# A hybrid decoder step: four experts of 32 slots on four column groups in one phase, decode attention on two column groups

## What is computed

```
s = jnp.einsum('nthe,nshe->nhts', qn_b, kn) + jnp.einsum('nthe,nse->nhts', qr_b, kr)
p = jax.nn.softmax(s, axis=-1).astype(ckv.dtype)
return jnp.einsum('nhts,nsr->nthr', p, ckv)
```

```
pg = softmax(xf @ moe_wg + moe_bg)                 # group: the first maximum
le = (xf @ moe_we + moe_be) per group              # top 2 of the 8 in the group
e_w = e_w / sum(e_w) * g_w
act = silu(einsum('md,edf->mef', xf, moe_w_gate)) * einsum('md,edf->mef', xf, moe_w_up)
y = einsum('mef,efd->md', act * comb[:, :, None], moe_w_down)
x = x + y
```

## Time and profile before

| what | us |
|---|---|
| median of 3 runs (lowest, highest) | 1697.03 (1689.72, 1700.62) |
| the profiled execution | 1686.48 |
| its span, first to last instruction | 1684.6 |
| TensorE busy in the span | 1491.5 |
| VectorE, ScalarE, GpSimd busy | 747.8, 387.4, 39.4 |
| L2230, gate and up matmuls of both layers, busy | 287.1 |
| L2264, down matmuls, busy | 146.2 |
| one layer's expert stage, 540.10 to 839.29 | 299.2 |

### The profile page before, as it was taken

The page is one execution under the profiler, slowest core; times in us unless marked ns, Lnnn a source line. Parts: engine busy times, 40 slices in busy tenths (PEclk is TensorE's granted clock), DMA queues, the critical chain, the costliest instruction groups (busy, mean ns, idle before and its releaser), DMA issues. The chain is left out here.

```text
span 1684.6 us, 22437 instructions
## 1 busy us (share of the span) xinstructions
PE 1491.5 (89%) x7812; PEld 980.9 (58%) x7812; DVE 747.8 (44%) x1544; ACT 387.4 (23%) x832; POOL 39.4 (2%) x46
## 2 busy tenths in 40 slices
PE   6988988969887899999889889789698878999997
PEld 3967577956566533333559675679465665333335
DVE  4675536473453322222446645373734533222224
ACT  1124313100212322222111243121003123222221
POOL 0040000000000000000001300000000000000000
PEclk9998999969999899999989989999699988999999
DMA  4461021125132899999135500212252338999991
GB/s 181 150 205 46 0 61 56 62 78 225 59 122 94 329 377 391 388 394 407 56 121 171 187 32 0 66 51 83 68 213 81 111 113 327 383 382 392 387 391 73
DMA packets 62313, 307.91 MB, mean 183 GB/s; under 512 B 13296, under 2 KB 16128, under 8 KB 35968
## 3 DMA queue, kind: packets, MB, share of 16 engines
q1 hardware_dynamic: 59136, 296.10, 46.1%
q0 software_dynamic: 3072, 10.49, 1.9%
HBM read 352.91 MB, written 3.98 MB: 212 GB/s over the span
## 5 line engine op out<-in xcount | busy, mean ns | idle before, releaser
L2230 PE MATMUL bank<-m_w,moe_hb 128*64 128x512 f32 x1280 | 287.1, 601 | 0.0
L509 PE MATMUL bank<-hT,wf 128*128 128x264 f32 x1024 | 251.0, 404 | 33.0 <-PEq L216 20.3
L509 PEld LDWEIGHTS bank<-hT,wf 128*128 128x128 f32 x1024 | 201.2, 200 | 75.3 <-issue 23.9
L2230 PEld LDWEIGHTS bank<-m_w,moe_hb 128*64 128x64 f32 x1280 | 89.1, 138 | 163.4 <-issue 162.7
L2328 DVE SCALAR_TENSOR_TENSOR tm<-bank,moe_scale,tm 128x256 f32<-128x256 f32 x40 | 19.4, 484 | 299.9 <-ACT tm L2300 299.9
L2347 DVE COPY m_YS<-bank 128x256 f32 x160 | 64.2, 422 | 51.7 <-issue 37.8
L2300 ACT ACTIVATE tm<-bank,moe_scale 128x256 f32<-128x256 f32 x40 | 19.0, 474 | 270.7 <-PE bank L2230 270.7
L2264 PE MATMUL bank<-m_w,tm 128*64 128x512 f32 x320 | 73.1, 598 | 0.9 <-ACT tm L2313 0.9
L2264 PE MATMUL bank<-moe_w,moe_aT 128*64 128x512 f32 x320 | 73.1, 598 | 0.0
L1784 PE MATMUL bank<-brT,wbr 128*128 128x264 f32 x256 | 60.7, 397 | 11.6 <-DMA wbr<-in_w_br 7.6
L288 PE MATMUL bank<-proj_hsp,proj_wsp 128*128 128x264 f32 x224 | 64.5, 288 | 1.9 <-DVE proj_wsp L282 1.9
(11 more groups left out here) (544 smaller groups left out, 2179.7 us busy)
## 6 DMA issues: line engine op xcount, KB each, us to landing
m_w<-in_w_x SPq DMA_DIRECT2D x200, 1024.0 KB, 10.5
moe_w<-in_w_x SPq DMA_DIRECT2D x40, 1024.0 KB, 7.0
wf<-in_w_gate SPq DMA_DIRECT2D x64, 512.0 KB, 3.6
proj_wfm<-in_w_fm SPq DMA_DIRECT2D x28, 512.0 KB, 4.3
wbr<-in_w_br SPq DMA_DIRECT2D x16, 512.0 KB, 3.6
mix_wo<-in_w_out SPq DMA_DIRECT2D x16, 512.0 KB, 4.1
mem_wkv<-in_w_kv SPq DMA_DIRECT2D x2, 2048.0 KB, 8.0
mem_ckT<-in_memkT SPq DMA_DIRECT2D x2, 2048.0 KB
```

The costliest lines, as they stand in the source:

```text
L509: mm = pe.matmul(E["bank"][to][:, 0:T], F["wf"][slot][:, k, :], E["hT"][:, k, :], start=k == 0, stop=k == KT - 1)
L2230: mm = pe.matmul(bank[s][W * g:W * g + W, :], hb[s][:, 4 * i + k, W * g:W * g + W], ring[s][i][g][:, COLS * k:COLS * k + COLS], start=i == ...
```

## The change

**Experts.** One phase "moe" takes the place of the three. W is 32, and a visit handles four experts on the four 32-column groups: 8 base visits and 16 spill slots in 4 spill visits, 12 in all, in the order b0 b1 b2 s0 b3 s1 b4 s2 b5 s3 b6 b7. The token columns are no longer gathered once for all, but for two visits at a time (`gather`, L2085: five matmuls for each of the 8 row blocks), and the result of a visit is multiplied by `Q` and added to the tokens at once, during the next visit (`combine`, L2142 and L2143, two matmuls for each of the 8 row blocks). Turning back, `YS`, `HS` and the combine phase are gone. A visit has six pieces, 0 to 3 for gate and up and 4 and 5 for down; a piece is half a tile (128 x 1024, 0.5 MiB) of each of the four experts, 2.10 MB. The ring has seven places of a piece, five for base pieces and two for spill pieces (the first seven base pieces use all). `plan()` gives each piece its place and sorts the loads by the piece that must be done before (`release`); below, (v, j) is piece j of visit v, so (4, 2) is piece 2 of the fifth visit, and visits 3, 5, 7 and 9 are the spill visits.

**Mix.** The first two pieces are loaded in the mix phase, into tiles that stay allocated.

**Attention.** The two halves of the decode scores go to two column groups (partitions 0 to 31 and 32 to 63), one matmul of each in turn; the latent's matmuls go to two groups by even and odd sequence, and VectorE adds the two sums. The same for scores and outputs of the memory attention.

```diff
-W = 64
+W = 32
 TILE = 2048
 SPILL = SLOTS // (W + 1)
-BASE_PAIRS, SPILL_PAIRS = NE // 2, SPILL // 2
-assert SPILL % 2 == 0
-HELD, FLAG = NE + SPILL, NE + 2 * SPILL
+BLOCKS = (T - 1) // W
...
+def pieces():
+
+    order = [(0, j) for j in range(4)]
+    for v in range(len(ORDER)):
+        if v + 1 < len(ORDER):
+            order += [(v + 1, j) for j in range(4)]
+        order += [(v, 4), (v, 5)]
+    return order
+
+
+PIECES = pieces()
+
+
+def plan():
+
+    home, loads, last, uses = {}, [], {}, {}
+    seen = {"base": 0, "spill": 0}
+    for at, (v, j) in enumerate(PIECES):
+        kind = ORDER[v][0]
+        n = seen[kind]
+        seen[kind] += 1
+        if kind == "spill":
+            slot = RING - SPILL_RING + n % SPILL_RING
+        else:
+            slot = n if n < RING else (n - RING) % (RING - SPILL_RING)
+        uses[slot] = uses.get(slot, 0) + 1
+        home[v, j] = (slot, uses[slot])
+        loads.append((last.get(slot, 0), at, v, j, slot))
+        last[slot] = at + 1
+    return home, [(v, j, slot, release) for release, at, v, j, slot in sorted(loads)]
+
+
+HOME, LOADS = plan()
...
-                mm = pe.matmul(bank[5][0:32, 0:MEM], qblk[:, i, :], ckT[:, i // 2, i % 2, :], start=i == 0,
-                               stop=i == 15)
+                g = i % 2
+                mm = pe.matmul(bank[5 - 3 * g][32 * g:32 * g + 32, 0:MEM], qblk[:, i, :], ckT[:, i // 2, g, :],
+                               start=i < 2, stop=i >= 14)
...
+            pe.wait_ge(S("gate_copied"), 7)
             for i in range(16):
-                mm = pe.matmul(bank[5][0:32, 0:256], pblk[:, i % 2, i // 2, :], cv[:, i // 2, i % 2, :],
-                               start=i == 0, stop=i == 15)
+                g = i % 2
+                mm = pe.matmul(bank[5 - g][32 * g:32 * g + 32, 0:256], pblk[:, g, i // 2, :], cv[:, i // 2, g, :],
+                               start=i < 2, stop=i >= 14)
...
-            step(nc.vector.tensor_reduce(mxs[:], bank[5][0:32, 0:MEM], AX.X, ALU.max))
-            step(nc.vector.tensor_scalar(scs[:], bank[5][0:32, 0:MEM], mxs[:], None, ALU.subtract), "shift_s",
-                 wait=False)
+            step(nc.vector.tensor_copy(scs[:], bank[2][32:64, 0:MEM]), "scs_copied")
+            step(nc.vector.tensor_tensor(scs[:], scs[:], bank[5][0:32, 0:MEM], ALU.add))
+            step(nc.vector.tensor_reduce(mxs[:], scs[:], AX.X, ALU.max))
+            step(nc.vector.tensor_scalar(scs[:], scs[:], mxs[:], None, ALU.subtract), "shift_s", wait=False)
...
-            for half in range(2):
-                for n in range(N):
+            for n in range(N):
+                for half in range(2):
                     at = PAGES * n + 4 * half
-                    mm = pe.matmul(bank[half][0:32, :], qblk[:, n, :],
+                    mm = pe.matmul(bank[half][32 * half:32 * half + 32, :], qblk[:, n, :],
                                    ckT[:, at:at + 4, :].rearrange("p a b -> p (a b)"), start=n == 0, stop=n == N - 1)
-                mm.then_inc(S("nope_done"), 1)
-                for g in range(2):
-                    mm = pe.matmul(bank[2 + half][0:32, :], qrblk[:, g, :],
+                    if n == N - 1:
+                        mm.then_inc(S("nope_done"), 1)
+            for g in range(2):
+                for half in range(2):
+                    mm = pe.matmul(bank[2 + half][32 * half:32 * half + 32, :], qrblk[:, g, :],
                                    krT[:, g, 4 * half:4 * half + 4, :].rearrange("p a b -> p (a b)"),
                                    start=g == 0, stop=g == 1)
-                mm.then_inc(S("rope_done"), 1)
-                if half == 0:
-                    pe.wait_ge(S("rinv_ready"), 1)
-                    for p in range(PAGES):
-                        mm = pe.transpose(bank[4 + p // 4][0:32, P * (p % 4):P * (p % 4) + P], ssq[:, p, :], ident)
-                    mm.then_inc(S("rT_done"), 1)
-                    pe.matmul(bank[6][0:32, 0:RANK], C("sel832")[0:N, :], ckvn[0:N, 2, :], start=True, stop=True)\
-                        .then_inc(S("rep_done"), 1)
+                    if g == 1:
+                        mm.then_inc(S("rope_done"), 1)
...
+            pe.wait_ge(S("own_copied"), 1)
             for p in range(PAGES):
                 pe.wait_ge(S("pblk_ready"), p + 1)
                 for n in range(N):
-                    i = N * p + n
-                    mm = pe.matmul(bank[5][0:32, 0:RANK], pblk[:, p, n, :], ck[:, n, RANK * p:RANK * p + RANK], start=i == 0,
-                                   stop=i == NPG - 1)
+                    i, g = N * p + n, n % 2
+                    mm = pe.matmul(bank[5 + g][32 * g:32 * g + 32, 0:RANK], pblk[:, p, n, :],
+                                   ck[:, n, RANK * p:RANK * p + RANK], start=i < 2, stop=i >= NPG - 2)
...
-            step(nc.vector.scalar_tensor_tensor(lat[:], own[:], sc[:, PAGES * P:], bank[5][0:32, 0:RANK], ALU.mult,
-                                                ALU.add))
+            step(nc.vector.tensor_copy(odd[:], bank[6][32:64, 0:RANK]))
+            step(tt(odd[:], odd[:], bank[5][0:32, 0:RANK], ALU.add))
+            step(nc.vector.scalar_tensor_tensor(lat[:], own[:], sc[:, PAGES * P:], odd[:], ALU.mult, ALU.add))
...
+            for v, j, slot, release in LOADS[:EARLY]:
+                at = slice(TILE // 2 * (j % 2), TILE // 2 * (j % 2) + TILE // 2)
+                for g in range(4):
+                    sp.dma_start(E["early"][slot][g][:], A["w_x"][l, 4 * ORDER[v][1] + g, j // 2][:, at])\
+                        .then_inc(S("early_loaded"), 16)
             for i in range(4):
                 sp.wait_ge(S("o_done"), i + 1)
                 sp.dma_start(wo[i][:], A["w_out"][l, 4 + i]).then_inc(S(f"wo{i}_loaded"), 16)
+            sp.wait_ge(S("early_loaded"), 64 * EARLY)
...
+            first_spill = True
+            for v, j, slot, release in LOADS[EARLY:]:
+                kind, b = ORDER[v]
+                i, at = j // 2, slice(HALF * (j % 2), HALF * (j % 2) + HALF)
+                if release:
+                    sp.wait_ge(S("piece_done"), release)
+                if kind == "spill" and first_spill:
+                    sp.wait_ge(S("items_ready"), 2)
+                    first_spill = False
+                for g in range(4):
+                    if kind == "base":
+                        sp.dma_start(ring[slot][g][:], A["w_x"][l, 4 * b + g, i][:, at]).then_inc(S(f"w{slot}_loaded"), 16)
+                    else:
+                        k = 4 * b + g
+                        e = sp.value_load(items[0:1, k:k + 1], min_val=0, max_val=NE - 1)
+                        used = sp.value_load(items[0:1, SPILL + k:SPILL + k + 1], min_val=0, max_val=1)
+                        sp.dma_start(ring[slot][g][:], A["w_x"][l, e, i][:, at], cond=used)\
+                            .then_inc(S(f"w{slot}_loaded"), 16)
...
+            def gate_up(v, j):
+                s, p, w = v % 2, v // 2, weights_here(v, j)
+                if j == 0 and v >= 2:
+                    pe.wait_ge(S("act_ready"), v - 1)
+                pe.wait_ge(S("hb_ready"), KT * p + 2 * j + 2)
+                for k in (2 * j, 2 * j + 1):
+                    for g in range(4):
+                        mm = pe.matmul(bank[s][W * g:W * g + W, :], hb[p % 2][:, k, P * s + W * g:P * s + W * g + W],
+                                       w[g][:, COLS * (k % 2):COLS * (k % 2) + COLS], start=k == 0, stop=k == KT - 1)
+                mm.then_inc(S("piece_done"), 1)
...
+            for v in range(N):
+                p = v // 2 + 1 if v % 2 == 0 and v + 2 < N else 0
+                for j in range(4):
+                    if v + 1 < N:
+                        gate_up(v + 1, j)
+                    for x in (2 * j, 2 * j + 1):
+                        if v:
+                            combine(v - 1, x)
+                        if p:
+                            gather(p, x)
+                    if j == 1:
+                        turn(v)
+                down(v, 0)
+                if p:
+                    slot_scales(p)
+                down(v, 1)
+            for d in range(KT):
+                combine(N - 1, d)
```

More of the change, by code:

```diff
@@ L1942, in route @@
[L1942 to L1948 removed]
+        table = ph.sb("table", [NE, 2, SPILL])
+        items = ph.sb("items", [1, 2 * SPILL], I32)
+        shifted = ph.sb("shifted", [P, 6, N])
@@ new lines, in moe, with done, base_slot @@
+        aT = [spare[:, 512:768].rearrange("p (f w) -> p f w", f=2), ph.sb("aT1", [P, 2, P])[:]]
+        high = ph.sb("high", [P, D_MODEL], F32R)
+        low = ph.sb("low", [P, D_MODEL], F32R)
+        ring = E["early"] + [[ph.sb(f"w{s}{g}", [P, HALF]) for g in range(4)] for s in range(EARLY, RING)]
+        LG, CNT, SLOT, XROW = 5, 6, 7, 1
+        PARTS = ((0, 0), (2, 0), (1, 1), (3, 1), (4, 2))
+        def done(v, j):
+            return PIECES.index((v, j)) + 1
+        def base_slot(v):
+            kind, b = ORDER[v]
```

(62 more changed lines are left out.)

641 lines of the change are left out of this document (224 added, 417 removed).

## The result

The changed kernel takes 1770.56 us, median of four (1767.48 to 1780.47), against 1694.36 for the kernel before (1689.72 to 1700.62): ratio 1.0453, 95% interval 1.0405 to 1.0502. It is 76 us slower, where 10 were forecast (1707 against 1697.03), and outside the range. The profiled execution is one of 1780.5 us.

A forecast was written before the change was run, and what follows sets the result against it. SyncE's conditional issues, with the DMA dry behind them, were taken to bound the stage: 2 x 20.9 - 31.6 = +10.2 us on 1686.5 gives 1696.7, and 10.5 from profiled execution to median gives 1707; range 1676 to 1750.

The forecast's parts named there:

- The step that failed: Expert stage: during 24 conditional issues, 37.7 us, the DMA has at most five base places, 27 us, so it runs dry.
- the sum: Expert stage per layer, first issue to tail along SyncE and DMA: 320.1 us against 299.2 before, +20.9.
- To the last issue of (4,2): Stage start: first issue 0.75, fourteen pieces at 381 GB/s 77.1, landing and one piece of work 3.9, issue 2.1 us.
- The 16 and the three cycles: Stage middle: 16 conditional issues 25.1 us, then three cycles of 24 conditional and 24 plain, 50.4 each, 151.2.
- The rest, nine pieces and the tail: Stage end: last nine pieces 49.5 us, first issue and landing 2.5, tail 7.9.
- Attention: Decode and memory attention on two column groups: 15.8 us less per layer, 31.6 for both layers.
- The two places filled early: Mix phase: loading two places, 4.2 MB or 11 us of DMA, costs nothing there.
- B: Rival, expert stage: spill issues are hidden and the DMA bounds it, 35 us less per layer, about 1595; chance 0.08.
- C: Rival, TensorE in the expert stage: four column groups overlap no more than two, visit 27.9 us, about 1797; chance 0.09.
- D: Rival, TensorE's clock in the expert stage: mean below 0.70 lengthens the cycles, 1728 to 1760, say 1746; chance 0.13.
- E: Rival, small gain: weights stream at 425 GB/s despite 4 KB rows and attention gives 33.4, 1679; chance 0.10.
- same: Whole kernel: the outcome of no measurable change, about 1%, 1680 to 1714 us; chance 0.46.

The follow-up runs named there:

- run 5: The changed kernel with expert weights laid out so a base piece is one load of 128 rows of 16 KB; 1696.01 us, ratio 1.0016.
- run 1: The changed kernel with a spill slot's expert number and flag read once per spill visit, not before each half tile; 1678.42 us, ratio 0.9940.
- run 2: The changed kernel without the conditional loads of the spill visits, the visits themselves still running; 1606.39 us, ratio 0.9522.
- run 8: The changed kernel with none of the ring's places filled during the mix (EARLY = 0); 1786.88 us, ratio 1.0563.
- run 10: The changed kernel with 16 KB rows, the list read once per visit, and spill visits after base visits 1, 3, 5 and 6; 1569.28 us, ratio 0.9297.
- run 7: The kernel before, each tile loaded in two halves of 128 rows of 4 KB, conditional loads doubled as well; 1689.82 us, ratio 0.9987.
- run 4: The changed kernel with one 2 MiB load (512 rows of 4 KB) for a base piece instead of four of 0.5 MiB; 1723.15 us, ratio 1.0230.

## Why the prediction was wrong

**The step that failed** is the one sentence on what the DMA has to do during a block of conditional issues, "the DMA has at most the five base places to fill, 10.5 MB, 27 us", with the sum's 24 plain loads at 0.53 each behind it. SyncE can't leave five places' loads behind: with loads of 128 rows of 4 KB the issue is held once about ten are outstanding, until one lands. The rate of 0.53 came from ten loads in a row, the most that its rows had. The places of the ring were taken for the depth of the queue, and the rows shown could not tell the two apart.

Against the sum, by SyncE's rows after:

- To the last issue of (4,2): 83.9 forecast, 530.92 to 625.65, 94.7 measured, +10.8. The sum let SyncE go on when 14 pieces had landed; but with ten loads as the most, 66 of the 76 must have landed, 16.5 pieces. Without the hold (run 5) the first conditional issue of the block comes after 86.2 us instead of 96.2. The rate was mis-sized the other way and hid a part: at the 408 GB/s measured the fourteen pieces take 72.0, not 77.1.
- The 16 and the three cycles: 176.3 forecast, 625.65 to 829.69, 204.0 measured, +27.7. The conditional block is as forecast, 37.8 for 37.7, and the plain loads take 22 of a cycle for 12.7. Without the hold the cycle is 51, as in the sum.
- The rest, nine pieces and the tail: 59.9 forecast, 61.7 measured.

Together 360.5 for 320.1, 40 a layer. Median to median the kernel lost 76 us where 10 were forecast, so the miss is 66, less than 80: the stage of layer 1 grew by 55.4 us from the start of the phase to the end of the span (305.2 to 360.6), that of layer 0 by 61.0, and the profiled executions lie 8 below and 10 above their medians.

**What held.** The mechanism, SyncE's conditional issues with the DMA dry behind them, was named and is shown by runs 1 and 2; what the forecast had too small was its size, by the hold. Attention: 31.1 for 31.6; decode attention 10.5 in layer 0 (87.8 to 77.3) for 10.8, the latent 8.82 for 8.5. The scores' exponential starts 15.8 us after the first score matmul, before 20.7: 4.8 for 4.4. In the memory attention the scores took 3.65, as forecast (3.5 to 4.0), and the outputs 4.45, at a granted clock of 0.83. The two places filled early: free in the mix (78.1 us with them, 80.3 without, run 8), 8 us a layer in the stage. Four column groups overlap nearly fully: a piece of 16 records takes 1.92, 0.12 each where 0.11 was ideal, against 0.22 on two groups. The scales were mis-sized: the sum had 0.8 a visit for turn and scales together, and the 12 small ones alone take 2.11, in every other visit. In all TensorE was busy 39 us in a cycle of run 1, at clock 0.89, for the 35.4 of the forecast.

**The rivals.** B (hidden): no, it decides at an issue of 0.85 us and the issue is 1.57. Run 1 has it at 0.36, and still isn't at B's 1595: the releases and the hold were in no rival. Run 10, with both corrections and another order, does get under it (1569). C: no, by the 1.92. D, the clock: it did fall, to a mean of 0.81 and 0.84 in the two cycles, 0.66 to 0.93 in the windows, and the piece of 678.85, right behind the wait of 11.34, ran at 0.50 (1.2 GHz) and took 3.64 instead of 1.92. The mean stayed over the 0.70 that D asked for, and TensorE was busy 41 of 60 us, so the clock looks like a result of the waits more than a cause. That is argued, not shown: how much it adds in the stretches where TensorE is waited for was not tried. E: the rate of the 4 KB rows was 408 in full windows, between the 381 taken and 425. The forecast of "same" rested on a gain and a loss of nearly one size; the gain was right (31), and the loss was 107 us (76 + 31) where 42 had been worked out.

## What to carry to other kernels

Before a list of loads is planned against ring places, find how many loads, and of how many rows, the issuing engine can leave outstanding; what is behind the last of them waits at the DMA's pace, and a slow issue after it starts late. Few long rows give the same bytes for less of that room. And price what an engine does per load (here two reads of a list, 1.2 us) by the number of loads after the change, not before it: cutting tiles in half and doubling the spill slots took it from 24 to 96 a layer. The forecast did price this, and run 2 shows that it is where most was to be had. The order of the visits was worth 59 us (run 10), about as much as either correction on top of the other (50 and 67): alternate the work so that neither the DMA nor TensorE has a stretch in which it waits for the other.

## What the runs showed of the hardware

- SyncE's issues were held with 10.2 loads of 128 rows of 4 KB outstanding (8.7 to 11.0 over the stage), 5.8 of 256, 3.5 of 512, and not with five of 128 rows of 16 KB, nor with 8.7 of 128 rows of 8 KB. A long issue alone doesn't show a full queue: in the trace of before the load of 460.42 took 2.18 us with at most three outstanding.
- The best windows (DMA share 1.03 with 4 KB rows, 1.00 and 1.01 with 16 KB rows) gave 408 to 411 GB/s in the changed kernel and 426 to 433 in run 5, above the 360 to 401 that the short windows of other phases had shown. In run 7, where the two halves of a tile follow each other, 4 KB rows gave 415 to 420. The Trainium skill, DMA: Bandwidth & Descriptors, Rules for kernel authors, wants at least 1 MiB a load for full bandwidth. By that rule the halves should have lost rate; here 0.5 MiB loads in 4 KB rows ran 4 to 6% under 2 MiB loads in 16 KB rows (1 to 4% in run 7), and 2 MiB loads in 4 KB rows (run 4, 409 to 411) no faster than the halves. So a larger load brought nothing and a longer row did; why run 7's halves ran faster was not tried.
- A conditional load that moves nothing takes SyncE 1.57 us with its two reads and 0.36 us without them, when no release is waited for; a read is 0.27 us and 0.26 more to check the value.
- Phases that the change doesn't touch differ between executions with the granted clock: the projection of layer 0 took 72.9 us in the profile before and 76.9 after, with the clock at 1.00 and 0.94 in the first 60 us.
